# First mixer: matrix powers on a dense form that ScalarE spreads, and scan and output projections in one block by channel halves

## The chip, the cores and the metric

The kernel runs on one core of a Trainium2 chip. The metric is the device time of one execution in microseconds. The program runs two transformer-like blocks over 256 tokens of width 2048; the change touches only the first mixer (S5), which fills the first tenth of the span.

## What is computed

The first mixer, cut to what matters (64 groups of 16 channels, 64 complex states for each group, 256 tokens):

```python
u, z = split(x @ w_in)                      # 2048 -> 2 x 1024
abar = exp(lam * dt)                        # complex, per group and state
bbar = (abar - 1) / lam * b                 # complex 64 x 16 per group
h[t] = abar * h[t-1] + bbar @ u[t]
y = real(c @ h) + d_skip * u
g = gelu(y)
y = g * sigmoid(g @ w_glu + b_glu)
return (y * silu(z)) @ w_out                # then x = layer_norm(alpha * x + ...)
```

## The kernel before

Every projection streams its weights from memory as *pieces* of 128x1024 f32 (512 KB), four to a *tile*. SyncE's queue (SP) loads a piece into one of 3 raw buffers (`stream`, L215) as soon as the difference of the piece three before it is made. ScalarE (ACT) casts it to the rounded half (`high`, L231), VectorE (DVE) forms the bf16 remainder (`low`, L237), and TensorE (PE) does three products for each (L264; L896 for the gate and output projections). 6 slots hold prepared pieces. All engines run their own instruction lists in program order; semaphores are the only tie between them, so the order of the work is the order in which it is written.

`s5_mixer_states` is one block. While PE multiplies the 8 tiles (32 pieces) of the input projection, DVE writes, between its `low` calls, the parameters, the matrices B, AB (`turn_by`, L735 to L740, six operations on 128x1024 each), and a table of cosines and sines that doubles in six steps (L793 to L798). B, A²B and A³B go through `b2`, one after the other: PE turns each (`turn(l)`, L595, 16 transposes into banks 4 to 7), ACT copies it out (`turned_out`, L547), and only then may DVE write the next power into `b2`. The four products of C with powers of A (`turn_conjugate`, L745 to L750) come after the last one. These matrices are block diagonal: a group has 16 channels and the layout gives each state tile 32 columns, so half of the 1024 columns of each part are zeros on either half of the partitions; they are multiplied all the same.

PE then makes `sums(0)` (L605), `kernels` (L619, needs three C powers), after ACT's eight copies of the result (L573, `m_copied`) `sums(1)`, and for each channel half h `direct(h)` (L628) and two `outputs(h, sp)` (L643). DVE runs four scan `unit(h, sp)` (L833 to L849) and two `skip(h)` (L856). A unit other than the first waits for `sums(1)` before it writes its states, since these lie where `sums` reads. The GELU (L580) of a half follows its outputs.

`s5_output` is a second block, behind a barrier of all engines: ACT rounds all of `gel` (L917), DVE forms its remainder (L942), PE does 2 tiles (8 pieces) of the gate projection, ACT the sigmoids (L928), DVE multiplies (L950), ACT rounds (L934), DVE takes the remainder (L952), and PE does 4 tiles (16 pieces) of the output projection. `x_rows` (2 MB, L904) is the first DMA of this block; the first 3 pieces of the gate projection have been loaded since the input projection's end. Layer norm follows in its own block.

Of the kernel before, what the change touches and what calls it, by code (L numbers as in the profile page):

```python
# [20 lines left out]
F32 = mybir.dt.float32  # L21
# [443 lines left out]
S5_GEL, S5_H0, S5_SMALL = 13312, 37888, 38912  # L465


def s5_mixer_states(k):
# [17 lines left out]
    tmp = k.at(S5_TMP, 1024)  # L486
    small = k.at(S5_SMALL, 64)
    k.s5 = dict(small=small)
# [3 lines left out]
    dt_ready, angle, trig, negated = (k.sem(n) for n in "dt_ready angle_ready trig_ready c_negated".split())  # L492
# [16 lines left out]
    with nc.Block() as block:  # L509
        @block.sync  # L510
        def _(sp):
            for n in range(PIECES):
                sp.dma_start(x_raw[:, n * 1024:(n + 1) * 1024],
                             ins["x_t"][:, n * 1024:(n + 1) * 1024]).then_inc(x_in[n], 16)
                if n < RAW:
                    sp.dma_start(k.raw(n), ins["weights"][n]).then_inc(k.landed[n], 16)
                    k.issued += 1
            k.stream(sp, AT_GLU)

        @block.scalar  # L520
        def _(act):
# [16 lines left out]
            for n in range(1, PIECES):  # L538
                high(act, n)
                k.high(act, n)  # L540
            act.wait_ge(bc_in, 64)
            nc.scalar.mul(ct[0][:, 1024:], ct[0][:, 1024:], -1.0).then_inc(negated, 1)
# [6 lines left out]
            for t in range(N_A_IN):  # L549
# [9 lines left out]
                nc.scalar.copy(dst, src).then_inc(k.bank_free, 1)  # L559
                if t == 4:  # L560
                    turned_out(0)
                if t == 6:
                    turned_out(1)
            turned_out(2)
            turned_out(3)
            act.wait_ge(m_sum, 1)
            for h in range(2):
                act.wait_ge(m_clear, h + 1)
                for s in range(4):
# [3 lines left out]
                    nc.scalar.copy(dst, src).then_inc(m_copied, 1)  # L573
            for h in range(2):
# [6 lines left out]
            act.wait_ge(gelu_done, 4)  # L581

        @block.tensor
        def _(pe):
            def turn(l):
# [3 lines left out]
                pe.wait_ge(powers, l + 1)  # L589
# [21 lines left out]
            def kernels():  # L611
                pe.wait_ge(c_powers, STEP - 1)
# [19 lines left out]
            def outputs(h, sp):  # L632
                u = 2 * h + sp
                pe.wait_ge(h_ready, u + 1)
                pe.wait_ge(c_powers, STEP)
# [12 lines left out]
                mm.then_inc(y_sum, 1)  # L648

# [15 lines left out]
            for h in range(2):  # L665
                pe.wait_ge(s_read, h + 1)
                direct(h)
                for sp in range(2):
                    outputs(h, sp)


        @block.vector
        def _(dve):
# [54 lines left out]
            r3 = lambda a: a.rearrange("p (i c) -> p i c", c=32)  # L728
            spread = lambda name: q[name].unsqueeze(2).to_broadcast([P, 32, 32])
            t3 = r3(tmp)  # L730

            def turn_by(out, src, re, im, signal=None):

                (o_r, o_i), (s_r, s_i) = ((r3(a[:, 0:1024]), r3(a[:, 1024:])) for a in (out, src))
                v(tt(o_r, s_r, spread(re), ALU.mult))  # L735
                v(tt(t3, s_i, spread(im), ALU.mult))
                v(tt(o_r, o_r, t3, ALU.subtract))
                v(tt(o_i, s_i, spread(re), ALU.mult))
                v(tt(t3, s_r, spread(im), ALU.mult))
                v(tt(o_i, o_i, t3, ALU.add), signal)  # L740

            def turn_conjugate(out, src, re, im):

                (o_r, o_n), (s_r, s_n) = ((r3(a[:, 0:1024]), r3(a[:, 1024:])) for a in (out, src))
                v(tt(o_r, s_r, spread(re), ALU.mult))  # L745
                v(tt(t3, s_n, spread(im), ALU.mult))
                v(tt(o_r, o_r, t3, ALU.add))
                v(tt(o_n, s_n, spread(re), ALU.mult))
                v(tt(t3, s_r, spread(im), ALU.mult))
                v(tt(o_n, o_n, t3, ALU.subtract), c_powers)  # L750

            dve.wait_ge(bc_in, 64)
            turn_by(bb, b2, "cr", "ci", powers)
# [24 lines left out]
            turn_by(b2, bb, "ar", "ai", powers)  # L778
            low(2)
# [8 lines left out]
            for n in range(6):  # L788
                m = 1 << n
                cc, ss = (q[x].unsqueeze(2).to_broadcast([P, 32, m]) for x in now)  # L790
                t = tmp[:, 0:32 * m].rearrange("p (i t) -> p i t", t=m)
# [7 lines left out]
                low(2 if n >= 3 else 1)  # L799
# [4 lines left out]
            dve.wait_ge(turned, 8)  # L804
            turn_by(b2, bb, "ar2", "ai2", powers)
            low(PIECES * N_A_IN)
            dve.wait_ge(negated, 1)
            v(nc.vector.tensor_copy(flat(q["wc"]), order(q["m4"])))
            dve.wait_ge(turned, 12)
            turn_by(b2, bb, "ar3", "ai3", powers)  # L810

            for d in range(1, STEP + 1):
                n = "" if d == 1 else str(d)
                turn_conjugate(ct[d], ct[0], "ar" + n, "ai" + n)
# [43 lines left out]

            unit(0, 0)
            skip(0)  # L860
            unit(0, 1)
            skip(1)
            unit(1, 0)
            unit(1, 1)


def s5_output(k):

    nc, ps = k.nc, k.ps
    gel, uz, small = k.at(S5_GEL, 2048), k.at(S5_UZ, 4096), k.s5["small"]  # L870
    z = uz[:, 2048:]
    sig, yy, sz = k.at(25600, 2048), k.at(27648, 2048), k.at(29696, 2048)
    gel_parts, yy_parts = k.split_x(35904, 0, 2048), k.split_x(36928, 2048, 2048)
    x, dst = k.at(8192, 4096), k.at(12288, 4096)
    xs, z_done, g_high, g_low, y_done, y_high, y_low, one = (k.sem(n) for n in (
        "x_rows z_silu g_high g_low y_gated y_high y_low glu_piece").split())

    def pieces(pe, first, n, parts, glu):

        for t in range(first, first + n):  # L880
            pe.wait_ge(k.bank_free, t + 1)
            for part in range(PIECES):
                piece = PIECES * t + part
                pe.wait_ge(k.low_done, piece + 1)
                for i, kk, sub in itertools.product(range(3), range(ECH // PIECES), range(4 if glu else 2)):
                    c = part * (ECH // PIECES) + kk
                    if glu:
# [1976 lines left out]
```

## Time and profile before

| | us |
|---|---|
| median of 3 runs | 3306.09 |
| lowest and highest | 3303.09, 3306.78 |
| the profiled execution | 3305.53 |
| its span in the trace | 3303.7 |
| PE, DVE, ACT busy over the span | 93%, 66%, 44% |

The profile's page gives the whole span; the mixer is seen in the windows by stage and in the timelines of the engines. Stages by the trace: input projection to 128 us, matrices and kernels to 172, scan and outputs to 232, gate projection to 272, output projection to 318.

### The profile page before, as it was taken

How to read it: one execution, taken by the hardware profiler on the slowest of the kernel's cores; microseconds unless marked ns; L12 is line 12 of the kernel's file. 1: busy time of each engine (PE TensorE's matmuls, PEld its weight loads, DVE VectorE, ACT ScalarE, POOL GpSimd, SP SyncE). 2: the span in 40 equal slices, each digit the busy share in tenths (PEclk: the TensorE clock that was granted, in tenths of full speed). 3: DMA queues.
4: the chain of work that ended last, by engine and by line, in shares of the span. 5: the costliest groups of instructions: out<-in, count | busy, mean ns of one | idle time of the engine just before them, and what ended most of it. 6: DMA issues, size and time to landing. Idle time of an engine off the chain costs nothing. (4 is left out here: it accounts for less than half of the span.)

```text
span 3303.7 us, 60290 instructions
## 1 busy us (share of the span) xinstructions
PE 3067.2 (93%) x23855; PEld 2517.0 (76%) x23922; DVE 2181.8 (66%) x3042; ACT 1466.8 (44%) x1933; POOL 29.8 (1%) x32
## 2 busy tenths in 40 slices
PE   7677899999988789999979989999999999999997
PEld 6674799988977678999869878777777777777654
DVE  8765544555555685575549999777777777777654
ACT  4223434565652443363434468444444444444443
POOL 0000000000000020000000000000000000000000
PEclk9878899999999899999989999999999999999999
DMA  5214556544435333353545532655566555655554
GB/s 200 77 52 153 199 160 185 166 135 141 139 120 169 128 122 97 116 170 111 178 154 175 175 128 93 215 193 192 186 200 192 191 191 193 198 191 192 191 195 149
DMA packets 143960, 529.90 MB, mean 160 GB/s; under 512 B 16992, under 2 KB 17760, under 8 KB 142048
## 3 DMA queue, kind: packets, MB, share of 16 engines
q1 hardware_dynamic: 140400, 510.33, 47.8%
q10 hardware_dynamic: 3312, 15.92, 1.3%
q8 instruction: 198, 3.24, 0.4%
q14 instruction: 50, 0.41, 0.0%
HBM read 521.99 MB, written 4.19 MB: 159 GB/s over the span
## 5 line engine op out<-in xcount | busy, mean ns | idle before, releaser
L237 DVE TENSOR_TENSOR mem<-mem,rounded 128x1024 bf16<-128x1024 f32 x952 | 1154.2, 1226 | 756.6 <-ACT rounded L231 748.6
L231 ACT CAST rounded<-mem 128x1024 fp32r<-128x1024 f32 x952 | 992.5, 1047 | 1395.4 <-PE ps L264 333.8
L264 PE MATMUL ps<-rounded 128*128 128x256 f32 x3328 | 474.1, 292 | 48.5 <-DVE mem L237 41.7
L264 PEld LDWEIGHTS ps<-rounded 128*128 128x128 f32 x3328 | 422.2, 193 | 53.7 <-issue 22.1
L264 PE MATMUL ps<-rounded,mem 128*128 128x256 bf16 x3328 | 445.5, 280 | 0.0
L264 PE MATMUL ps<-mem,rounded 128*128 128x256 bf16 x3328 | 431.7, 277 | 13.8 <-DVE mem L237 13.8
L264 PEld LDWEIGHTS ps<-mem,rounded 128*128 128x128 bf16 x3328 | 320.7, 99 | 62.8 <-DVE mem L237 8.7
L264 PEld LDWEIGHTS ps<-rounded,mem 128*128 128x128 bf16 x3328 | 316.4, 98 | 62.0 <-issue 1.4
L2444 PE MATMUL ps<-rounded 128*128 128x512 f32 x1024 | 335.3, 441 | 2.1 <-DVE mem L2718 2.1
L2708 DVE TENSOR_TENSOR mem<-mem,ps 128x512 f32<-128x512 f32 x392 | 268.4, 685 | 69.2 <-PE ps L2444 62.5
L2444 PE MATMUL ps<-mem,rounded 128*128 128x512 bf16 x969 | 294.6, 381 | 3.7
L2375 PE MATMUL ps<-rounded 128*128 128x256 f32 x2048 | 288.8, 289 | 8.9 <-ACT mem L2545 3.8
L2375 PE MATMUL ps<-rounded,mem 128*128 128x256 bf16 x2048 | 276.8, 276 | 0.0
L2375 PEld LDWEIGHTS ps<-rounded 128*128 128x128 f32 x2048 | 259.9, 190 | 18.3 <-issue 6.4
L2444 PE MATMUL ps<-rounded,mem 128*128 128x512 bf16 x1016 | 271.2, 387 | 0.5
L2375 PE MATMUL ps<-mem,rounded 128*128 128x256 bf16 x2048 | 247.5, 273 | 1.6 <-DVE mem L237 1.6
L2444 PEld LDWEIGHTS ps<-rounded 128*128 128x128 f32 x1024 | 189.7, 189 | 57.2 <-DVE mem L2718 2.5
L2375 PEld LDWEIGHTS ps<-mem,rounded 128*128 128x128 bf16 x2048 | 199.8, 98 | 27.9 <-DVE mem L237 2.7
L2375 PEld LDWEIGHTS ps<-rounded,mem 128*128 128x128 bf16 x2048 | 187.0, 96 | 36.4
L2444 PEld LDWEIGHTS ps<-rounded,mem 128*128 128x128 bf16 x1024 | 98.8, 97 | 126.5
L2444 PEld LDWEIGHTS ps<-mem,rounded 128*128 128x128 bf16 x1024 | 78.8, 97 | 137.1 <-issue 70.8
L337 PE MATMUL ps<-mem 128*128 128x128 f32 x96 | 18.6, 384 | 72.0 <-DVE mem L422 50.2
(409 smaller groups left out, 2436.8 us busy)
## 6 DMA issues: line engine op xcount, KB each, us to landing
mem<-experts SPq DMA_DIRECT2D x512, 512.0 KB, 3.6
mem<-weights SPq DMA_DIRECT2D x440, 512.0 KB, 3.6
mem<-x_t SPq DMA_DIRECT2D x4, 512.0 KB, 10.1
mem<-x_rows SPq DMA_DIRECT2D x1, 2048.0 KB, 7.5
mem<-ln_g ACTq DMA_DIRECT2D x2, 1024.0 KB, 5.1
mem<-ln_b ACTq DMA_DIRECT2D x2, 1024.0 KB, 7.4
mem<-cmp_w_k ACTq DMA_DIRECT2D x4, 512.0 KB, 5.5
mem<-cmp_w_v ACTq DMA_DIRECT2D x4, 512.0 KB, 4.9
```

What stands on the lines that cost most here:

```text
L231: self.nc.scalar.copy(self.parts(c % SLOTS)[0], self.raw(c % RAW)).then_inc(self.high_done, 1)
L237: self.nc.vector.tensor_tensor(wl, self.raw(c % RAW), wh.bitcast(F32), ALU.subtract).then_inc(self.low_done, 1)
L264: mm = self.nc.tensor.matmul(self.ps[:, bank, half * 256:half * 256 + 256], a, b, start=(part == 0 and n == 0), stop=(part == PIECES - 1 a ...
L337: mm = nc.tensor.transpose(ps[:, b, c * T + tt * P:c * T + tt * P + P], src[:, tt * D + kc * P:tt * D + kc * P + P], self.ident)
L2375: mm = nc.tensor.matmul(ps[:, bank, half * T:half * T + T], a, b, start=(part == 0 and n == 0), stop=(part == PIECES - 1 and n == len(KIND ...
L2444: mm = nc.tensor.matmul(ps[:, bank, :], a, b, start=(j <= WITH_UP and half == 0 and i == 2 * tt), stop=((j < WITH_UP or j == PAIRS - 1) an ...
L2708: nc.vector.tensor_tensor(y[:, a:a + BANK], y[:, a:a + BANK], ps[:, bank, :], ALU.add).then_inc(y_free, 1)
```

## The change

Both functions become one, `s5_mixer`, with one block.

1. **Dense powers.** ACT packs B once and C once into 128x512 a part (`make_dense`, 4 copies of 64x512 each). `turn_by(n)` works on that form, six operations on 128x512, for all eight products: n = 0 and 1 are B and AB, 2 to 5 the four C powers, 6 and 7 A²B and A³B. ACT spreads a result to its place in the wide form (`expand(n)`, 4 copies of 64x512). Two buffers `dense` alternate; from n = 3 on `turn_by(n)` waits until spread n - 2 is done. GpSimd (POOL) clears the five targets that no DMA has filled, once, at the start.
2. **Placement.** The C powers are made inside the table's loop, each followed by two `low` calls, with one instead of one or two before it; spreads stand on ACT behind the drains of tiles 2 to 6.
3. **Waits.** PE's `turn`, `kernels` and `outputs` wait for spreads (`expanded`) instead of DVE's results.
4. **One block by halves.** GELU, rounding, remainder, gate and remainder of the gated product are done for half the channels at a time; a piece of the gate or output projection waits only for the half that it reads. Preparation of the first pieces moves between the units and GELUs. `x_rows` and all pieces behind the first three are issued after the last unit (`h_ready` 4).

```diff
+            def expand(n):
+                act.wait_ge(dense_ready, n + 1)
+                if n == 0:
+                    act.wait_ge(cleared, 5)
+                for l, at_ in ((2, 6), (3, 7)):
+                    if n == at_:
+                        act.wait_ge(turned, 4 * l)
+                for part in range(2):
+                    for f in range(2):
+                        last = nc.scalar.copy(own(SPREADS[n], part, f), dense_of((dense[n % 2], b_dense)[n == 0], part, f))
+                last.then_inc(expanded, 1)
...
+                if t == 1:
+                    make_dense(c_dense, ct[0], c_in_dense)
+                if t == 2:
+                    expand(0)
+                if t == 3:
+                    expand(1)
                 if t == 4:
                     turned_out(0)
+                    expand(2)
+                if t == 5:
+                    expand(3)
                 if t == 6:
                     turned_out(1)
+                    expand(4)
+                    expand(5)
+                    expand(6)
             turned_out(2)
+            expand(7)
             turned_out(3)
...
+            more(3)
+            act.wait_ge(s_sum, 2)
+            nc.scalar.activation(sz, z, ACT.Silu).then_inc(z_done, 1)
             for h in range(2):
                 act.wait_ge(y_sum, 2 * h + 2)
...
+                act.wait_ge(gelu_done, 2 * h + 2)
+                nc.scalar.copy(half(gel_parts[0], h), half(gel, h)).then_inc(g_high, 1)
+                if h == 0:
+                    more(3)
...
-                pe.wait_ge(powers, l + 1)
+                pe.wait_ge(expanded, (1, 2, 7, 8)[l])
...
-                pe.wait_ge(c_powers, STEP - 1)
+                pe.wait_ge(expanded, 5)
...
+                        pe.wait_ge(k.low_done, piece + 1)
+                        pe.wait_ge(low, 1 + part // 2)
...
+        @block.gpsimd
+        def _(pool):
+            for a in (bb, ct[1], ct[2], ct[3], ct[4]):
+                nc.gpsimd.memset(a, 0.0).then_inc(cleared, 1)
...
+            def turn_by(n, src, re, im, conjugate=False):
+                out = (dense[n % 2], b_dense)[n == 0]
+                if n > 2:
+                    dve.wait_ge(expanded, n - 1)
...
-                low(2 if n >= 3 else 1)
+                low(1)
+                if n >= 2:
+                    c_power(n - 1)
+                    low(2)
...
+            for h in range(2):
+                dve.wait_ge(g_high, h + 1)
+                tt(half(gel_parts[1], h), half(gel, h), half(gel_parts[0], h).bitcast(F32), ALU.subtract).then_inc(g_low, 1)
+                more(3 if h == 0 else 2)
...
+            sp.wait_ge(h_ready, 4)
+            sp.dma_start(rows, ins["x_rows"]).then_inc(xs, 16)
+            k.stream(sp, AT_KV)
```

ACT's list at the end of the input projection, before the change (L559 drains a tile, L547 is `turned_out`):

```order
58 L559 COPY mem<-ps 128x512 [waits multiplied]
59 L547 COPY mem<-ps 128x512 [waits b_turned] x4
60 L559 COPY mem<-ps 128x512 [waits multiplied]
61 L547 COPY mem<-ps 128x512 [waits b_turned] x8
62 L573 COPY mem<-ps 32x16x32 [waits s5_kernels_clear,s5_kernels_sum]
```

and after it (L604 drains, L592 is `turned_out`, L582 spreads):

```order
69 L604 COPY mem<-ps 128x512 [waits multiplied]
70 L592 COPY mem<-ps 128x512 [waits b_turned] x4
71 L582 COPY mem<-mem 64x32x16 [waits dense_ready]
72 L582 COPY mem<-mem 64x32x16 x3
73 L582 COPY mem<-mem 64x32x16 [waits dense_ready]
74 L582 COPY mem<-mem 64x32x16 x3
75 L582 COPY mem<-mem 64x32x16 [waits b_turned,dense_ready]
76 L582 COPY mem<-mem 64x32x16 x3
77 L604 COPY mem<-ps 128x512 [waits multiplied]
78 L592 COPY mem<-ps 128x512 [waits b_turned] x4
79 L582 COPY mem<-mem 64x32x16 [waits b_turned,dense_ready]
```

Three spreads now stand between the drain of tile 6 and that of tile 7, and a fourth between the copies of the third and the fourth turned matrix.

DVE's list behind the last `low` of the input projection, before (one operation stands for its group of six; four groups L745 to L750 follow one another):

```order
161 L237 TENSOR_TENSOR mem<-mem,rounded 128x1024 [waits high_done] x4
162 L808 COPY mem<-mem 128x32 [waits c_negated]
163 L735 TENSOR_TENSOR mem<-mem 128x1024 [waits b_turned,vector_step]
...
169 L745 TENSOR_TENSOR mem<-mem 128x1024 [waits b_powers]
...
192 L750 TENSOR_TENSOR mem<-mem 128x1024 [waits vector_step]
193 L817 COPY mem<-mem 128x2048 [waits b_turned,c_powers]
```

and after:

```order
182 L237 TENSOR_TENSOR mem<-mem,rounded 128x1024 [waits high_done] x3
183 L856 TENSOR_TENSOR mem<-mem 128x512 [waits expanded]
...
189 L926 COPY mem<-mem 128x32 [waits dense_ready]
190 L856 TENSOR_TENSOR mem<-mem 128x512 [waits expanded,vector_step]
...
196 L931 COPY mem<-mem 128x2048 [waits b_turned,expanded,dense_ready]
```

Thirty operations on 128x1024 behind the last `low` have become twelve on 128x512.

ACT's list around the two GELUs after the change (L649 rounds a half of `gel`, L231 casts pieces):

```order
92 L647 ACTIVATE mem<-ps 128x2x4x64 [waits s5_y_sum]
93 L647 ACTIVATE mem<-ps 128x2x4x64
94 L649 CAST rounded<-mem 128x1024 [waits s5_gelu]
95 L231 CAST rounded<-mem 128x1024 [waits multiplied,piece_landed_2]
96 L231 CAST rounded<-mem 128x1024 [waits multiplied,piece_landed_0]
97 L231 CAST rounded<-mem 128x1024 [waits multiplied,piece_landed_1]
98 L647 ACTIVATE mem<-ps 128x2x4x64 [waits s5_y_sum]
```

The second GELU stands behind the casts of three pieces whose DMAs are issued behind `x_rows`.

## Rows read from the trace of the kernel before

**Rows 1.** Windows by stage: length, busy time of each engine (instructions), clock, DMA.
```profile
0.00:128.00 128.00, 102.73 (x816) 90.28 (x816) 97.34 (x171) 50.74 (x62) 0.20 (x4) 0.95 0.52 179
128.00:172.00 44.00, 17.39 (x401) 16.35 (x400) 41.84 (x35) 5.46 (x10) 0.00 (x0) 0.71 0.00 1
172.00:232.00 60.00, 55.57 (x928) 55.05 (x928) 43.08 (x52) 7.49 (x10) 0.00 (x0) 0.70 0.01 2
```
**Rows 2.** Timeline of PE, 126 to 240 us: start, length, instruction, idle before.
```profile
126.14 1.91 PE L595 MATMUL ps<-mem 128*128 128x128 f32 x16
135.74 3.68 PE L595 MATMUL ps<-mem 128*128 128x128 f32 x16 [7.68 <-DVE mem L740]
140.09 7.37 PE L605 MATMUL ps<-mem 32*128 32x64 f32 x256 [0.67 <-ACT mem L547]
158.50 6.29 PE L619 MATMUL ps<-mem 128*32 128x128 f32 x128 [11.04 <-DVE mem L750]
174.62 13.93 PE L605 MATMUL ps<-mem 32*128 32x64 f32 x256 [9.82 <-ACT mem L573]
188.48 17.33 PE L628 MATMUL ps<-mem 128*128 128x64 f32 x80
205.74 8.29 PE L643 MATMUL ps<-mem 128*32 128x64 f32 x256
...
223.03 7.15 PE L643 MATMUL ps<-mem 128*32 128x64 f32 x256
```
**Rows 3.** Timeline of DVE: power, table step, last C power, units.
```profile
29.11 1.22 DVE L735 TENSOR_TENSOR mem<-mem 128x1024 f32<-128x1024 f32 x1
...
77.00 0.69 DVE L793 TENSOR_TENSOR mem<-mem 128x512 f32<-128x512 f32 x1
...
164.68 1.23 DVE L750 TENSOR_TENSOR mem<-mem 128x1024 f32<-128x1024 f32 x1
...
171.67 1.16 DVE L833 TENSOR_TENSOR mem<-ps,mem 128x1024 f32<-128x1024 f32 x1
...
183.75 1.22 DVE L833 TENSOR_TENSOR mem<-ps,mem 128x1024 f32<-128x1024 f32 x1
...
216.34 0.68 DVE L849 TENSOR_TENSOR mem<-mem 128x504 f32<-128x504 f32 x1
```
**Rows 4.** Timeline of ACT: drains, copies of turned matrices and of kernels.
```profile
54.28 0.58 ACT L559 COPY mem<-ps 128x512 f32<-128x512 f32 x1
...
119.13 0.58 ACT L559 COPY mem<-ps 128x512 f32<-128x512 f32 x1
119.61 2.05 ACT L547 COPY mem<-ps 128x512 f32<-128x512 f32 x4
...
169.70 4.78 ACT L573 COPY mem<-ps 32x512 f32<-32x512 f32 x8 [29.66 <-DVE mem L819]
```
**Rows 5.** Timelines, gate and output projections: first and last groups.
```profile
238.28 2.05 PE L896 MATMUL ps<-rounded 128*128 128x256 f32 x8 [8.09 <-DVE mem L237]
...
242.87 1.19 PE L896 MATMUL ps<-rounded 128*128 128x256 f32 x8
...
261.30 1.03 PE L896 MATMUL ps<-mem,rounded 128*128 128x256 bf16 x8
271.58 2.08 PE L896 MATMUL ps<-rounded 128*128 128x512 f32 x4 [9.25 <-DVE mem L952]
...
316.40 1.07 PE L896 MATMUL ps<-rounded,mem 128*128 128x512 bf16 x4
```
**Rows 6.** The page, DMA issues: count, KB each, us from issue to landing.
```profile
mem<-weights SPq DMA_DIRECT2D x440, 512.0 KB, 3.6
...
mem<-x_rows SPq DMA_DIRECT2D x1, 2048.0 KB, 7.5
```
**Rows 7.** Timeline of POOL, the shortest and the longest operation there.
```profile
1143.02 0.61 POOL L1911 TENSOR_TENSOR mem<-mem 128x255 f32<-128x255 f32 x1
...
1174.45 2.54 POOL L1911 TENSOR_TENSOR mem<-mem 128x255 f32<-128x255 f32 x1
```

More of the change, by code:

```diff
@@ L573, in _, with more @@
                     nc.scalar.copy(dst, src).then_inc(m_copied, 1)
+            ahead = iter(range(G0, G0 + N_GA))
+            def more(n):
+                for _, c in zip(range(n), ahead):
+                    k.high(act, c)
+            more(3)
+            act.wait_ge(s_sum, 2)
+            nc.scalar.activation(sz, z, ACT.Silu).then_inc(z_done, 1)
             for h in range(2):
@@ L580, in _ @@
                     nc.scalar.activation(dst, src, ACT.Gelu_apprx_tanh).then_inc(gelu_done, 1)
-            act.wait_ge(gelu_done, 4)
+                act.wait_ge(gelu_done, 2 * h + 2)
+                nc.scalar.copy(half(gel_parts[0], h), half(gel, h)).then_inc(g_high, 1)
+                if h == 0:
+                    more(3)
+            for n in range(N_GLU):
+                more(4 if n == 0 else 2)
+                t = AT_GLU + n
+                act.wait_ge(k.multiplied, PIECES * (t + 1))
+                for sub in range(4):
+                    j = 4 * n + sub
+                    last = nc.scalar.activation(sig[:, j * T:(j + 1) * T],
+                                                ps[:, t % BANKS + 3 * (sub // 2), (sub % 2) * T:(sub % 2) * T + T],
+                                               ACT.Sigmoid, bias=small[:, 8 + j:9 + j])
+                    last.then_inc(k.bank_free if sub == 3 else sig_done, 1)
+                act.wait_ge(y_done, n + 1)
+                nc.scalar.copy(half(yy_parts[0], n), half(yy, n)).then_inc(y_high, 1)
+            more(N_GA)
         @block.tensor
@@ L777, in _ @@
             low(2)
-            turn_by(b2, bb, "ar", "ai", powers)
-            low(2)
+            turn_by(1, b_dense, "ar", "ai")
+            low(3)
             order = lambda a: a.rearrange("p (h j s) -> p h s j", h=2, s=4)
@@ L857, in skip, with more @@
                                                      op0=ALU.mult, op1=ALU.add), m_ready if j % 4 == 3 else None)
+            ahead = iter(range(G0, G0 + N_GA))
+            def more(n):
+                for _, c in zip(range(n), ahead):
+                    k.low(dve, c)
             unit(0, 0)
@@ L1409, in first_block @@
 def first_block(k):
-    s5_mixer_states(k)
-    s5_output(k)
+    s5_mixer(k)
     h = k.at(12288, 4096)
```

201 lines of the change are left out of this document (85 added, 116 removed).

## The prediction

> **What bounds the kernel now.** I read the windows by stage first [rows 1]. In the input projection (to 128 us) PE is busy 102.7 of 128 us at a clock of 0.95, and DVE 97.3. From 128 to 172 us PE works 17.4 of 44 us while DVE works 41.8: this stage is DVE's. From 172 to 232 PE works 55.6 of 60 us, at a mean clock of 0.70. The timelines of PE name the holes and who ends them [rows 2]: 7.7 us on the last B power, 11.0 us on the third C power, 9.8 us on the copies of the kernels, and behind the scans 8.1 us on the first pieces of the gate projection and 9.3 us on the remainder of the gated product [rows 5]. The 9.8 us is DVE's too: the copies sat 29.7 us waiting for a memset [rows 4] that stands behind the last C power, which ends at 165.9 us [rows 3].
>
> **1. The powers, up to the end of the input projection.** A power is six operations of 1.22 us, 1.26 us from start to start, so 7.6 us; on 128x512 one takes 0.69 us in the same 32x16 shape with a broadcast operand [rows 3], with the same gap 0.73, so 4.4 us. Ahead of the last `low` DVE had three powers, 22.7 us, and gets six, 26.2 us: +3.5 us of DVE work. Against it stand blocks of 4.4 instead of 7.6 us, which drain PE's prepared pieces less. The two exceptions are the table's last step, now with only one `low` before the next power, and the spreads on ACT. A spread is four copies; the nearest row is four copies of 128x512 in 2.05 us [rows 4]. They lie in ACT's idle time (50.7 busy of 128 us, [rows 1]). I take the last product of the projection at 126.1 us as before, with -4 to +5 us as bounds: minus 4 where the shorter blocks pay, plus 5 for the added DVE work and one more restart at the low clock. POOL's five memsets lie ahead of the first spread and cost nothing here.
>
> **2. From there to `sums(1)`.** New waits come: PE's third turn waits for spread 6. ACT drained tile 6 at 119.1 us and copied four banks in 2.05 us to 121.7 [rows 4]. Spreads 4 and 5 follow to 123.7 and 125.8. DVE's A²B waits for spread 4, its buffer, and takes 4.4: 128.1. Spread 6 ends at 130.2, so the third turn starts there and not at 126.1. PE has idled 4 us; after 7.7 us of idling the same 16 transposes took 3.68 instead of 1.91 us [rows 2], and I take 3.7: 133.9. The last bank is copied at 134.5, spread 7 ends at 136.6, the fourth turn takes 3.7 to 140.3, its last copy 0.7: `sums(0)` starts at 141.1, against 140.1. Up to here the change has lost 1.0 us.
>
> Now the gain. `sums(0)` takes 7.4 us as in its row, to 148.5. The C powers are long spread, so `kernels` follows with no wait. It took 6.29 us after an idle stretch; `sums` shows what the clock makes, 7.37 or 13.93 us [rows 2]. In that ratio full speed is 3.3 us; I take 3.6, with 6.3 as the other end: 152.1. DVE has only a copy and three memsets between its last power (132.5) and the units, so the memsets are done by 146. The eight copies take 4.8 us [rows 4]: `sums(1)` starts at 157.0 instead of 174.6. **Gain 17.6 us.**
>
> **3. `sums(1)` to the last outputs.** Before, this chain is PE's alone: one operation behind the other from 174.62 to 223.03 + 7.15 = 230.2 us, while DVE's last unit ended at 217.0 [rows 2, 3]. PE's idle time ahead of it shrinks from 9.8 to 4.9 us. I take the same durations, which gives 157.0 + 55.6 = 212.6. DVE must not be later: a unit and a skip take 183.75 - 171.67 = 12.1 us [rows 3]. The first unit starts at 148.5; the second, from 160.6, must wait for the end of `sums(1)` at 170.9 before it writes, and ends at 172.6; its skip, three new `low` calls (3.5 us) and two units of 10.5 us end at 198.7. PE wants the last one at about 209. Covered by 10 us.
>
> **4. The hole before the gate projection.** PE goes on at 212.6 with pieces 32 and 33, whose remainders are ready, for 5.5 us, to 218.1. The second half's GELU (2.1), rounding (1.0) and remainder (1.2) end at 217.0. This needs ACT free at 212.6. It stands in three casts whose pieces are issued behind `x_rows` at 198.7. `x_rows` took 7.5 us for 2 MB and a piece lands 3.6 us after its issue [rows 6]. The four transfers are 3.5 MB; in proportion 13.1 us, at best 7.5 + 3 x 1.2 = 11.1. I take 12 and a cast of 1.0: ACT is free at 211.7, by a margin of 0.9 us. So the hole of 8.1 us goes, and with it the restart: the projection took 238.28 to 262.3, 24.0 us [rows 5], of which its last seven pieces took 242.87 to 262.3, 2.78 us each. Eight at that rate take 22.0 with the tail counted once, so the low clock at its start cost 2.0. **Gain 8.1 + 2.0 = 10.1 us**; the gate ends at 234.6.
>
> **5. The hole before the output projection.** The first half's gated product is made while PE does the second gate tile. The second half needs, from 234.6, four sigmoids (1.6), product (1.2), rounding (1.0) and remainder (1.2), 5.2 us with the signals; PE has pieces 40 and 41 to do, 5.4 us. The cover is whole by 0.2 us, and a miss costs what it misses. The output projection took 271.58 to 317.47, 45.9 us, for 16 pieces [rows 5]; at the same price of a restart, 2.0, it takes 43.9 without. **Gain 9.3 + 2.0 = 11.3 us.** It ends at 278.5. Layer norm and all behind it are unchanged and shift as they are. The barrier between the two old blocks was part of the 8.1 us.
>
> Sum: 17.6 + 10.1 + 11.3 = 39.0 us from the profiled execution's 3305.5 (0.6 below the median of the runs): **3266.5 us.**
>
> **The rivals.** *A, the sum as above*, 0.52, within 3262 to 3270.
>
> *B, the clock returns during `sums(1)`.* In the trace PE ran `sums(1)` and `direct(0)` for 31 us without a pause at half speed (13.93 against 7.37, 17.3 us), and sped up in the outputs [rows 2]. If the shorter idle stretch leaves the clock up, PE waits for DVE instead: the units end at 197.4, the outputs at 201.0. But the second GELU still waits for the three pieces, to 210.4; its remainder is there at 214.8, PE has idled 8 us and restarts low, and the end is 277.2: 3265.2. The 11 us that PE gains there are worth 1.3. Chance 0.12. The Trainium skill (TensorE: Matmul & The Clock Gate, Part 1: The HAM clock gate) says that sustained matmul activity releases the low clock soon after its start; the rows of `sums(1)` and `direct(0)` speak against it. By that rule the time would be this rival's.
>
> *C, the clock is low in `sums(0)`.* The third and fourth turns now stand apart, each after a pause, where one pair stood before. If the clock has not risen by 141 us, `sums(0)` takes 13.9 and `kernels` 5.3: +8.2 us on everything behind, 3275. Chance 0.14.
>
> *D, the fetch behind `x_rows` is late.* If the four transfers take 16 us, ACT is free at 215.7, PE stops for 2.5 us and may restart low: 3270 to 3272. Chance 0.08.
>
> *E, the input projection gets longer*, by the 3.5 us of DVE work and spreads that hold back casts, plus a low restart: 3271 to 3274. Chance 0.09.
>
> *F, slower: POOL's memsets.* Spread 0 waits for all five and stands on ACT at 54.8 us [rows 4]; behind it are the casts of tile 4 and so the whole projection. Five clears of 2048 columns have no row. From operations on 255 columns in 0.61 to 2.54 us [rows 7], eight times as wide: 24 to 102 us together. Up to 54 us they are free; beyond, each us delays all. At 93 us, 18.6 us each, the gain is gone; at 102 us the result is 3314. Those rows have two operands to read and a memset has none, so I stay near the short end. Chance 0.03. The Trainium skill (SBUF — State Buffer, Who interferes with whom) says that a DVE operation with two inputs contends with GpSimd operations that read, and not with ones that only write; no run shown here has both, and by it the clears disturb nobody.
>
> The last 0.02 is for a spread that costs far more than its row.
>
> **How the numbers follow.** A and B are the two likeliest and lie together. C, D and E reach to 3275. Bounds: 4 us off the projection below, 5 above. The range 3257 to 3277 leaves out F and the sums of two mishaps, some 2 in 10. About 0.2% is what a measurement of this kernel can tell from no change, 7 us: even C is 31 us below the old time. Faster 0.95, within 0.2% 0.02, slower 0.03.
>
> **What the new profile would show.** PE's first `sums` near 141 us and `kernels` right behind it; the second near 157, at half the clock; no gap over 1 us between the last outputs and the last product of the output projection, at about 278.5. A gap in the third and fourth gate pieces means B or D; `sums(0)` of 14 us means C; POOL busy beyond 54 us means F. I am wrong in kind if DVE's `low` calls wait for ACT's spreads in the projection, for which the last product there would lie beyond 131 us.

## The result, and the profile after

The changed kernel takes 3271.95 us (median of 4 runs, 3266.00 to 3273.36) against 3306.44 us before (4 runs, 3303.09 to 3309.07): a ratio of 0.9896, 95% interval 0.9884 to 0.9908. It is faster by 34.5 us where 39.0 were forecast; the forecast time was 3266.5, its range 3257 to 3277. The profiled execution took 3271.05 us, its span is 3269.3.

The timeline of PE after the input projection, columns as in [rows 2]:

```profile
132.52 3.61 PE L678 MATMUL ps<-mem 128*128 128x128 f32 x16 [6.34 <-ACT mem L582]
139.33 3.62 PE L678 MATMUL ps<-mem 128*128 128x128 f32 x16 [3.20 <-ACT mem L582]
143.63 11.65 PE L688 MATMUL ps<-mem 32*128 32x64 f32 x256 [0.68 <-ACT mem L592]
155.21 5.99 PE L702 MATMUL ps<-mem 128*32 128x128 f32 x128
166.20 13.93 PE L688 MATMUL ps<-mem 32*128 32x64 f32 x256 [4.99 <-ACT mem L631]
180.06 17.33 PE L711 MATMUL ps<-mem 128*128 128x64 f32 x80
...
215.12 7.15 PE L726 MATMUL ps<-mem 128*32 128x64 f32 x256
222.20 1.21 PE L753 MATMUL ps<-rounded 128*128 128x256 f32 x8
...
244.20 1.17 PE L753 MATMUL ps<-rounded 128*128 128x512 f32 x4
```

Where PE stood 7.7 us ahead of the fourth turn and 11.0 ahead of `kernels` [rows 2], it now stands 6.3 and 3.2 ahead of the third and fourth turn and not at all ahead of `kernels`; the 9.8 us ahead of `sums(1)` are 5.0; those of 8.1 and 9.3 us ahead of the two projections [rows 5] are gone. But `sums(0)` takes 11.65 us where it took 7.37. The windows of that stretch say why (from:to, length, busy time of PE, PEld, DVE, ACT, POOL, granted clock of PE, DMA):

```profile
144.00:146.00 2.00, 2.00 (x80) 2.00 (x80) 1.41 (x3) 0.00 (x0) 0.00 (x0) 1.00 0.04 8
146.00:148.00 2.00, 2.00 (x49) 2.00 (x48) 1.62 (x2) 0.00 (x0) 0.00 (x0) 0.55 0.00 0
148.00:160.00 12.00, 12.00 (x234) 11.70 (x233) 5.43 (x6) 0.00 (x0) 0.00 (x0) 0.51 0.01 3
160.00:164.00 4.00, 1.21 (x44) 0.94 (x34) 3.90 (x4) 2.64 (x5) 0.00 (x0) 0.91 0.00 0
164.00:200.00 36.00, 33.80 (x388) 33.60 (x390) 30.83 (x40) 9.39 (x10) 0.00 (x0) 0.50 0.01 1
...
202.00:222.00 20.00, 20.00 (x488) 19.84 (x485) 10.18 (x11) 6.23 (x6) 0.00 (x0) 1.00 0.52 192
```

The clock (0.5 is 1.2 GHz, 1.0 is 2.4) fell at 146 us, in the middle of `sums(0)`, while PE was fully busy. It stayed at half through `sums(1)` and `direct(0)`, 36 us with PE busy for 33.8 of them, and was full again at 202.

ScalarE's timeline shows the price of a spread (four copies of 64x512, L582), what stands ahead of the spreads, and how the second GELU stands behind the three late casts:

```profile
119.72 1.05 ACT L231 CAST rounded<-mem 128x1024 fp32r<-128x1024 f32 x1 [5.63 <-DMA mem<-weights]
120.67 0.58 ACT L604 COPY mem<-ps 128x512 f32<-128x512 f32 x1
121.15 2.05 ACT L592 COPY mem<-ps 128x512 f32<-128x512 f32 x4
123.06 5.04 ACT L582 COPY mem<-mem 64x512 f32<-64x512 f32 x8
129.97 2.50 ACT L582 COPY mem<-mem 64x512 f32<-64x512 f32 x4 [1.86 <-DVE mem L861]
...
220.10 1.05 ACT L231 CAST rounded<-mem 128x1024 fp32r<-128x1024 f32 x1 [0.18 <-DMA mem<-weights]
222.32 2.02 ACT L647 ACTIVATE mem<-ps 128x512 f32<-128x512 f32 x2 [1.17 <-PE ps L726]
```

Tile 6 is drained at 120.67 us, behind the cast of a piece whose load ended late; before the change it was drained at 119.13 [rows 4].

Last, POOL's five clears, against which [rows 7] had to serve as a bound:

```profile
0.74 8.77 POOL L787 MEMSET mem<- 128x2048 f32 x5 [0.29 <-POOLq L2904]
```

| PE, us | before | forecast | after |
|---|---|---|---|
| input projection ends | 126.1 | 126.1 | 126.1 |
| third turn starts | 126.1 | 130.2 | 132.5 |
| `sums(0)` starts, length | 140.1, 7.4 | 141.1, 7.4 | 143.6, 11.65 |
| `kernels`, length | 6.3 | 3.6 | 6.0 |
| `sums(1)` starts | 174.6 | 157.0 | 166.2 |
| last outputs end | 230.2 | 212.6 | 222.3 |
| gate projection ends | 262.3 | 234.6 | 244.2 |
| output projection ends | 317.5 | 278.5 | 288.0 |

### The profile page after: what moved, and what is told of

The parts are those of the page before. It is cut to its first block and busy times, and to the rows that moved or that the text cites. A ratio compares the mean times of both kernels' runs of the same rounds, so it can differ in the third digit from the quotient of the medians.

```text
span 3269.3 us, 60355 instructions
## 1 busy us (share of the span) xinstructions
PE 3063.5 (94%) x23855; PEld 2516.6 (77%) x23922; DVE 2158.3 (66%) x3046; ACT 1490.4 (46%) x1975; POOL 38.6 (1%) x37
## 3 DMA queue, kind: packets, MB, share of 16 engines
q8 instruction: 198, 3.24, 0.4%
## 5 line engine op out<-in xcount | busy, mean ns | idle before, releaser
L231 ACT CAST rounded<-mem 128x1024 fp32r<-128x1024 f32 x952 | 991.8, 1047 | 1376.5 <-PE ps L264 335.3
L264 PEld LDWEIGHTS ps<-mem,rounded 128*128 128x128 bf16 x3328 | 318.6, 99 | 66.0 <-DVE mem L237 17.5
L337 PE MATMUL ps<-mem 128*128 128x128 f32 x96 | 17.0, 358 | 70.0 <-DVE mem L422 48.6
```

The lines of the kernel that those rows point to most:

```text
L231: self.nc.scalar.copy(self.parts(c % SLOTS)[0], self.raw(c % RAW)).then_inc(self.high_done, 1)
L264: mm = self.nc.tensor.matmul(self.ps[:, bank, half * 256:half * 256 + 256], a, b, start=(part == 0 and n == 0), stop=(part == PIECES - 1 a ...
L337: mm = nc.tensor.transpose(ps[:, b, c * T + tt * P:c * T + tt * P + P], src[:, tt * D + kc * P:tt * D + kc * P + P], self.ident)
```

## The experiments

**One part alone.** `powers_only` keeps the old order of blocks and takes the new powers; `halves_only` the reverse.

```diff
 powers_only: s5_mixer with the dense powers, spreads and clears; then, in a block of its own as before,
+    s5_output(k)
 halves_only: one block by halves, powers on 128x1024 by VectorE alone
-            make_dense(dense[1], b2, b_in_dense)
...
-            r3 = lambda a: a.rearrange("p (i c) -> p i c", c=16)
+            r3 = lambda a: a.rearrange("p (i c) -> p i c", c=32)
```

> Powers in the dense form, with spreads, as in the changed kernel; the output stage is the old one, a block of its own behind a barrier. Theory (the two parts add): PE's timeline up to the last outputs is that of the changed kernel (first sums near 143.6 us and 11 to 12 us long, last outputs ending near 222.3), then the two old holes of 8.1 and 9.3 us and the two restarts at the low clock, 21.4 us together: 21.4 us above the changed kernel's 3272.0, 3293.4. Rival 1: the 4.9 us by which the changed kernel's profiled execution is ahead of what its mixer saves belong to run-to-run differences; then this one gains only the 7.9 us of the earlier last outputs on 3306.4: 3298.5. Rival 2: the spreads and added waits bring nothing without the halves: 3306.

> The old wide powers on VectorE, with no spreads and no memsets on GpSimd; scan and output stage in one block by halves, as in the changed kernel. Theory (fetch coupling): last outputs end near 230.2 us; VectorE's last unit ends at 217.0 plus 3.5 for three new differences, 220.5, x_rows is issued there, its three followers have landed and been cast 13.2 us later at 233.7, so the second GELU starts 3.5 us after its sums are ready and the third gate piece waits 2.4 us: 21.4 less 2.4 gained, 3287.4. Rival: the fetch does not matter, 21.4 gained, 3285.0, with no gap in the gate projection. Rival 2: the halves were worth less and the rest came from the powers: above 3292.

Powers alone: 3297.62 us (8 runs, 3289.39 to 3300.98), ratio 0.9970 (0.9958 to 0.9982). Halves alone: 3282.89 us (4 runs, 3280.62 to 3283.51), ratio 0.9931 (0.9914 to 0.9947). The two ratios multiply to 0.9901, and both parts together have 0.9896: within the intervals the parts add. The powers alone came out 4.2 us above their theory (3293.4) and near their first rival; the halves alone 2.1 below the rival that the fetch does not matter (3285.0), and their gate projection runs without a gap. Timeline of PE with the powers alone:

```profile
144.22 13.93 PE L659 MATMUL ps<-mem 32*128 32x64 f32 x256 [0.67 <-ACT mem L588]
158.08 5.40 PE L673 MATMUL ps<-mem 128*32 128x128 f32 x128
168.44 13.93 PE L659 MATMUL ps<-mem 32*128 32x64 f32 x256 [4.97 <-ACT mem L627]
...
232.30 2.04 PE L978 MATMUL ps<-rounded 128*128 128x256 f32 x8 [8.09 <-DVE mem L237]
```

Here `sums(0)` ran wholly at half clock, the powers gained 6.2 us instead of 17.6, and the old hole of 8.09 us stands as it was. The eight runs lie in two groups, three at 3289.4 to 3291.2 and five at 3295.6 to 3301.0; the mean clock was 0.962 to 0.964 in the first three and 0.960 in the four longest. That is the size of what the clock does to `sums(0)` and `kernels`, up to 8.2 us by the prediction's rows, but only one of the eight has rows, so this reading is argued, not shown. The halves alone went from last outputs at 232.2 to a gate's end at 254.1: the time from the last outputs to the layer norm's transposes (L337, which start at 339.25 us before the change) was 109.1 us before, 87.8 with the halves alone and 87.2 in the changed kernel. The prediction's steps 4 and 5 said 21.4 less; it is 21.3 and 21.9.

**Keeping the clock up.** Transposes of the identity into a free bank, in PE's pauses: 76 ahead of `sums(0)`, or 40 ahead of `sums(1)`.

```diff
 fill_sums0
+            filler(50)
             turn(2)
+            filler(26)
             turn(3)
 fill_sums1
             pe.wait_ge(k.bank_free, AT_A_IN + N_A_IN + BANKS)
+            filler(40)
             pe.wait_ge(m_copied, 8)
             sums(1)
```

> The changed kernel with 76 needless 128x128 transposes of the identity into a free bank, 50 ahead of the third turn and 26 ahead of the fourth, so that PE doesn't pause there (the result is unaffected). Theory 1 (the pauses before it made the clock fall in the first sums): the turns take 1.9 us each, sums(0) starts near 140.3 us and takes 7.4, kernels 3.6, sums(1) starts near 156.2: 10 us gained, 3262. Theory 2 (the products of sums, 32 rows deep, do not hold the clock, whatever ran before): sums(0) starts near 140.3 but its second part is again at half the clock, 9 to 12 us in all, kernels 6: 2 to 5 us gained, 3267 to 3270.

> The changed kernel with 40 needless 128x128 transposes between kernels and sums(1), where PE pauses 5.0 us. Theory 1 (the pause brings the clock down): sums(1) takes 7.4 us and direct(0) 9.1 instead of 13.9 and 17.3, the last outputs then wait for VectorE's units, and the second GELU for its three casts: last outputs 10 us earlier, but a hole in the gate projection; end 1 to 5 us earlier. Theory 2 (sums doesn't hold the clock): sums(1) starts at full speed and loses it on the way, 9 to 12 us, direct(0) at half speed, 17.3: last outputs 2 to 5 us earlier.

Ahead of `sums(0)`: 3287.32 us (2 runs), 15 slower than the changed kernel. Ahead of `sums(1)`: 3271.29 (2 runs), no difference. Both times mislead. Windows of the first, then PE's timeline of the second:

```profile
126.00:140.00 14.00, 12.48 (x112) 11.92 (x110) 8.44 (x13) 11.11 (x20) 0.00 (x0) 1.00 0.01 1
140.00:142.00 2.00, 1.17 (x38) 1.02 (x39) 1.31 (x2) 0.93 (x2) 0.00 (x0) 1.00 0.00 0
...
144.00:154.00 10.00, 10.00 (x192) 9.85 (x192) 3.04 (x3) 0.00 (x0) 0.00 (x0) 0.50 0.01 2
```

```profile
143.79 7.37 PE L688 MATMUL ps<-mem 32*128 32x64 f32 x256 [0.68 <-ACT mem L592]
...
159.76 7.37 PE L688 MATMUL ps<-mem 32*128 32x64 f32 x256 [0.38 <-ACT mem L631]
167.06 9.14 PE L711 MATMUL ps<-mem 128*128 128x64 f32 x80
...
217.98 2.05 PE L753 MATMUL ps<-rounded 128*128 128x256 f32 x8 [6.76 <-DVE mem L994]
```

In the first the clock was full from 126 to 142 us and still fell early in `sums(0)` (11.66 us), as its theory 2 had it. But that theory's reason, that the products of `sums` do not hold the clock, falls with the second kernel, where `sums(0)` and `sums(1)` both ran in 7.37 us. There all is at full clock from 144 to 200, `direct(0)` took 9.14 us, and the outputs ended 16.8 us earlier, at 205.5. Not all of that is the fillers' work: `sums(1)` began 6.4 us earlier than in the changed kernel, because `sums(0)` and `kernels` ahead of the fillers, whose code is the same in both, ran at full clock in this execution. Some 10 us are left for the fillers. Then the gate projection stopped for 6.8 us on the second half's remainder, whose GELU stands behind the late casts; the layer norm's transposes came 8.3 us earlier (301.1), and 1.4 earlier in the first kernel. Up to here neither kernel is later than the changed one, but the first lost 16 us and the second 8 somewhere behind 310 us.

**Where the fillers' time went.** Both lost most of it (15.0 and 6.3 us) between the pauses of PE at 2001.5 and 3077.3 us (in the changed kernel's time), in the expert stage, where the same code runs. The timeline of PE in that stage, of `fill_sums0`:

```profile
2289.92 1.22 PE L2427 MATMUL ps<-rounded 128*128 128x256 f32 x8 [1.03 <-issue]
2293.19 0.86 PE L2427 MATMUL ps<-rounded,mem 128*128 128x256 bf16 x6 [1.81 <-issue]
```

"issue" is a wait for nothing that the profile shows; such waits come back once per expert, every 133 us. The next two kernels add 40 or 128 small transposes (32x32) in the middle of the input projection:

```diff
             turn(0)
+            pad(40)    # or pad(128)
```

> The changed kernel with 40 small transposes (32x32, into a PSUM bank that nothing uses then) on TensorE behind the turning of B, in the middle of the input projection, where TensorE waits for VectorE anyway. What is computed stays the same. It asks why the kernels with fillers lost time in the expert stage, 1500 us behind the fillers: between the pauses at 2001.5 and 3077.3 the changed kernel takes 1075.8 us, the one with 40 fillers ahead of the second sums 1082.1, the one with 76 fillers 1090.8, and there TensorE stands still for 1 to 2 us, with no releaser, once per expert. Theory P: what counts is where TensorE's later instructions lie in its stream; 40 more matmuls (80 instructions) shift them as before, so the stretch takes 1080 to 1084 us and shows such pauses, and the whole 3275 to 3279 us. Theory Q: the fillers' place and kind made it (they ran beside the first mixer's end, and changed when later transfers start): here the stretch takes 1075 to 1077 us and the whole 3269 to 3273.

> The same with 128 small transposes in place of 40, at the same place: 256 more instructions in TensorE's stream. One expert's work is 1152 matmuls, 2304 instructions or 9 times 256, and the pauses came back at one place of each expert; if the stream is loaded in blocks of 256 instructions, a shift by 256 puts every later instruction where it was. Theory P (place in the stream, in blocks of 256): the stretch in the expert stage takes 1075 to 1077 us again and has no such pauses, the whole 3269 to 3273 us. If more instructions cost more of themselves, the stretch takes over 1090 and the whole over 3285. Theory Q: 1075 to 1077 too, so this run tells P from 'more is worse', and the run with 40 tells P from Q. The 128 transposes take 3.5 to 7 us of TensorE beside pauses of 28.9 us in all: nothing of it should reach the projection's end at 126.1.

They took 3271.25 us (3267.17 and 3275.33) and 3268.39 (3264.35 and 3272.44). The two runs of each lie 8 us apart, too far to tell one theory from the other. The stretch in the trace, from one execution of each kernel, tells more:

| instructions added on PE | stretch in the expert stage, us |
|---|---|
| none (before, changed, five others here) | 1075.8 to 1077.9 |
| 80 (`fill_sums1`, `pad40`) | 1082.1, 1079.9 |
| 152 (`fill_sums0`) | 1090.8 |
| 256 (`pad128` and three below) | 1076.6 to 1077.7 |

`pad40` has the waits again, `pad128` none of 0.9 us or more:

```profile
2554.23 1.21 PE L2425 MATMUL ps<-rounded 128*128 128x256 f32 x8 [1.22 <-issue]
```

So with 80 or 152 more instructions ahead of it the unchanged stage took 2 to 15 us more, and with 256 more it did not: what counts is the place of PE's later instructions in its stream, not how many were added. Of these rows `pad40` is weak, since it lies 2.0 us above the unshifted kernels, one execution of it has a trace, and `powers_only` and `rows_twice`, which add nothing, have such waits too, of up to 1.0 us. A second sign of the place is a pause in the last outputs, shown below with `rows_twice`. That it is the loading of instructions in blocks fits, but is not shown. The page has a queue for it (`q8 instruction`, 198 packets, 3.24 MB), with 199 packets in all four kernels with 256 more but 200 in `fill_sums0`; no row ties a packet to a wait, and the block could as well be a divisor of 256. With 256 in all (`fill_pad`: 40 ahead of `sums(1)`, `pad(88)` in the projection):

> The changed kernel (powers in its own order) with the 40 transposes ahead of the second sums and 88 small ones behind the turning of B, 256 instructions in all. It separates the two things that the run with 40 alone mixed: its output projection ended 8.2 us earlier, its expert stage took 6 us more. Theory: granted clock 1.00 from 144 to 200, gate projection done at 236, expert stretch 1076 to 1078 us, and the whole 3262 to 3266 us, 6 to 10 us under the changed kernel. Rival: the gain of the clock is given back elsewhere whatever the place in the stream, and the whole stays within 3 us of 3271.

3267.05 us (4 runs, 3263.08 to 3268.16), ratio 0.9882 (0.9865 to 0.9898), 4.9 less than the changed kernel and between its theory and its rival; the runs of the two kernels overlap. `sums(0)` was at half clock this time (13.93 us), `sums(1)` at full (7.37). The outputs ended at 209.5, 12.8 us earlier, the gate projection at 242.4, only 1.8 earlier. This is rival B's price: PE's gain is held by the three pieces behind `x_rows`.

**The load of `x_rows`.**

```diff
+            for o in (S5_TMP, S5_B2):
+                sp.dma_start(k.at(o, 2048), ins["x_rows"][:, 0:2048]).then_inc(xs, 16)
             sp.dma_start(rows, ins["x_rows"]).then_inc(xs, 16)
```

> The changed kernel with two more loads of 1 MB (halves of x_rows, into buffers that are free by then and that nothing reads) ahead of the load of x_rows; VectorE waits for all three where it waited for x_rows. It asks whether the load of x_rows, which stands ahead of the gate projection's weight pieces 35 to 37 in the queue, is really hidden, and by how little. In the changed kernel those pieces are cast at 217.6 to 221.1, the second GELU, queued behind them on ScalarE, ends its wait with 1.2 us to spare, and the gate projection runs without a gap. Two more MB at the rate of x_rows itself (2 MB in 7.4 us) put the pieces about 7 us later. Theory: the second GELU and the low part of its halves follow, the gate projection stops for 5 to 6 us between its second and third pieces and starts again at the lower clock, and the whole takes 5 to 8 us more than the changed kernel: 3277 to 3280 us. Rival: the pieces have slack that the profile doesn't show, and the whole stays within 2 us of 3272.

3275.53 us (4 runs, 3275.30 to 3278.38), 3.6 more: between both. ScalarE cast the first of the three pieces 5.4 us later:

```profile
222.97 1.04 ACT L231 CAST rounded<-mem 128x1024 fp32r<-128x1024 f32 x1 [13.56 <-DMA mem<-weights]
```

But the gate projection did not stop for it, since PE came late too, by a pause in the last outputs, while 4 MB were being fetched:

```profile
224.50 0.82 PE L728 MATMUL ps<-mem 128*32 128x64 f32 x17 [2.55 <-issue]
```

Three more kernels have this pause, and its place tells of PE's stream. It stands 17 matmuls before the end of the outputs in `rows_twice` (2.55 us) and `halves_only` (1.61), 93 before it in `fill_sums0` (1.21), which has 76 more ahead, and 57 before it in `pad40` (0.21), which has 40 more ahead: at one place by count, wherever that falls in the code. Why it is longest beside the larger fetch was not tested.

In `rows_twice` it made the outputs end 3.0 us later and the gate projection, restarted at the low clock, take 1.3 us more. So the margin of 1.2 us was neither used up nor proved; the extra traffic cost what it did in another way.

**An order without the pauses.** The table above shows 17.5 us between the projection and `sums(0)`, all of them two spreads, two turns and their copies. `early` brings A²B and A³B forward: nothing is computed anew. The edit, condensed and without VectorE's part:

```diff
-    SPREADS = (bb, b2, ct[1], ct[2], ct[3], ct[4], b2, b2)
+    SPREADS = (bb, b2, b2, ct[1], b2, ct[2], ct[3], ct[4])
 ScalarE, behind the drain of tile 4, 5, 6
+                if t == 4: turned_out(0); turned_out(1); expand(2)
+                if t == 5: expand(3); turned_out(2); expand(4)
+                if t == 6: turned_out(3); expand(5); expand(6)
 TensorE
+            for l in range(1, STEP):
+                k.multiply(pe, AT_A_IN + 3 + l, 1, xT, "channel")
+                turn(l)
+            k.multiply(pe, AT_A_IN + 7, 1, xT, "channel")
```

> The changed kernel with the powers in another order: A2B right behind AB, then AC, A3B, A2C, A3C, A4C; ScalarE spreads A2B and A3B during tiles 4 and 5 and copies out every turned power as it comes; TensorE turns one power behind each of tiles 4, 5 and 6, in place of the last two behind the projection. The same numbers are computed. Theory: the 17.5 us from the projection's end at 126.1 to the first sums at 143.6 were the wait for two spreads (6.3 and 3.2), two turns at the lower clock (3.6 each) and their copies (0.7), all of which now lie inside the projection, whose last wait for VectorE is at 114.97. Projection's end 126 to 129 (two turns of 1.9 us are now inside it), first sums at 127 to 130, that is 14 to 16.5 us earlier; VectorE's first unit starts when the sums are done, at 135 to 141 in place of 155.3, and since what follows is the chain sums, kernels, sums, outputs, the last outputs end 14 to 19 us earlier (203 to 208) and the whole takes 3253 to 3259 us. Rival: the casts and low parts of the weights, which the spreads now delay on ScalarE, hold the projection back: its end moves to 132 or later, the whole to 3262 or more. Rival 2: the projection is followed by the sums without a pause and the clock behaves otherwise: full through sums and kernels, 6.6 us less than that, or half from the start, 2.3 us more.

3248.34 us (4 runs, 3246.86 to 3249.26), ratio 0.9821 (0.9804 to 0.9837), 23.6 less than the changed kernel:

```profile
126.29 7.37 PE L688 MATMUL ps<-mem 32*128 32x64 f32 x256
133.59 3.77 PE L702 MATMUL ps<-mem 128*32 128x128 f32 x128
142.33 13.93 PE L688 MATMUL ps<-mem 32*128 32x64 f32 x256 [4.97 <-ACT mem L631]
```

`sums(0)` now follows the projection without a pause, 17.3 us earlier and at full clock; the outputs end at 198.3, the gate projection at 220.2. It gained more than its theory, because the clock held in `sums(0)` and `kernels`: that is its rival 2, which put 6.6 us on it. Three more kernels add the fillers (40 and 88), a later load of `x_rows`, or both:

```diff
 x_rows behind the gate projection's pieces
-            k.stream(sp, AT_GLU)
+            k.stream(sp, AT_A_OUT)
             sp.wait_ge(h_ready, 4)
             sp.dma_start(rows, ins["x_rows"]).then_inc(xs, 16)
```

> The kernel with the earlier powers, with 40 transposes of 128x128 ahead of the second sums, where TensorE waits 5 us for ScalarE's copies of the kernels (they kept the granted clock at 1.00 all through the sums, the direct part and the outputs in the earlier run with them, where those ended 16.8 us earlier), and 88 small transposes behind the turning of B, so that 256 instructions in all are added to TensorE's stream and the expert stage is left as it was by the theory of blocks of 256. Theory: clock full from the second sums on, last outputs no longer bound by TensorE at half clock but by VectorE's units, end of the gate projection 224 to 228 (235.96 with the 40 alone, less the 10 to 14 us that the units start earlier), expert stretch 1075 to 1077; the whole 3247 to 3254 us. Rivals: the gate projection is held by its weights and VectorE's low parts and ends as in the kernel with earlier powers alone, the whole within 2 us of it; or the clock falls in the first sums and stays low in spite of the fillers: the same, within 2 us.

> The kernel with earlier powers and both kinds of transposes, with one more change: SyncE issues the gate projection's weight pieces 35 to 42 first, as their slots come free, and waits for the scan and loads x_rows behind them. In the two earlier kernels pieces 35 to 37 were cast at 195 us in both, though TensorE had finished the outputs at 198.3 in one and 191.0 in the other: they stood behind the wait for VectorE's last unit (184.8) and the 7.4 us of x_rows, and so the gate projection ended at 220.2 and 221.4. Theory: the pieces' slots are free at 164, they are cast before 175, the gate projection starts at 191 and runs without a gap, 22.0 us, to 213, 8 us earlier; x_rows is issued by about 205 and there long before the output projection's first end at 237; the whole takes 3240 to 3244 us. Rival: the output projection's own pieces (eight of 512 KB, fetched over 38 us) are held by the load of x_rows, which now falls among them, and give 3 to 8 us of it back: 3244 to 3250 us.

> The kernel with earlier powers and the load of x_rows behind the gate projection's pieces, without any transposes added. The transposes alone gave nothing (3249.4 against 3248.3 us), both together 8.5 us (3239.8). Theory: without them TensorE does the second sums and the first direct part at the lower clock and finishes the outputs at 198.3, when pieces 35 to 37 are cast in either order, so the gate projection ends at 220.2 as before and the whole takes 3247 to 3249 us: the two cuts are worth something only together. Rival: the load's place is worth its 8 us by itself, 3240 us, and the transposes do nothing.

| | median (4 runs), us | outputs end | gate projection ends |
|---|---|---|---|
| `early` | 3248.34 | 198.3 | 220.2 |
| `early_fill` | 3249.40 | 191.1 | 221.4 |
| `early_rows` | 3249.09 | 199.8 | 221.7 |
| `early_fill_rows` | 3239.84 (3239.21 to 3240.73) | 191.4 | 213.3 |

Either alone is worth nothing, both together 8.5 us. `early_fill` came out as its rival had it, the other two as their theories did, within 0.2 us of their ranges. With the fillers alone ScalarE's casts of pieces 35 to 37 are late; with both they are there, and the load of `x_rows`, which lands in 9.4 us, is issued 30 us before VectorE first reads it (230.3). First ScalarE of `early_fill`, then ScalarE and SyncE's queue of `early_fill_rows`:

```profile
195.08 1.05 ACT L231 CAST rounded<-mem 128x1024 fp32r<-128x1024 f32 x1 [24.71 <-DMA mem<-weights]
```

```profile
170.58 2.93 ACT L231 CAST rounded<-mem 128x1024 fp32r<-128x1024 f32 x3
...
199.88 0.42 SPq L543 DMA_DIRECT2D mem<-x_rows  x1
```

`early_fill_rows` beats both kernels: ratio 0.9803 (0.9786 to 0.9819) to the one before, 32 us less than the changed one. What binds it now is VectorE's last unit (PE waits 4.8 us for it ahead of the last outputs).

## Why the prediction was right, and where its steps were not

The forecast was 5.4 us too low, and the mechanism was the one that it named: PE's holes in front of the chain and in front of the two projections went. Its largest term was not right, and part of what that term missed came back by a gain that nobody had forecast.

**Step 1** held for the end of the input projection, 126.1 us. Over the first 126 us VectorE was busy for 102.3 us where it had been 97.3, more than the 3.5 us expected. PE was busy for 97.1 instead of 100.7, at a mean clock of 0.97 instead of 0.95, so it ran less of its work at the low clock. That shorter blocks did this fits, but no run separates them. The spreads fit into ScalarE's idle time.

**Step 2** is where the 9.2 us by which `sums(1)` was late come from, in three terms. First, `sums(0)` started 2.5 us late. Of this 1.4 us was there before any spread began, since the drain of tile 6 stood behind a late cast and came at 120.67 us instead of 119.1. Most of the rest is the spreads: each was sized by four copies of 128x512 from PSUM, 2.05 us, and four of 64x512 within SBUF took 2.50. Second, `sums(0)` was taken at 7.4 us and was 11.65 (+4.3). Third, `kernels` was taken at 3.6 and was 5.99 (+2.4, close to the other end, 6.3). Rival C named the last two, with a chance of 0.14 and a price of 8.2 us; they came to 6.7. Its mechanism was that the clock has not risen by 141 us. It had risen (1.00 from 144 to 146) and fell again in a busy stretch, which no rival held. In `powers_only`, whose code up to there is the same, it had not risen. The gain of the step was 8.4 us, not 17.6.

**Step 3** held in all its durations: 166.2 + 56.1 = 222.3, where 55.6 were taken. VectorE was covered: its second unit waited 3.9 us for `sums(1)`, as the step said it would. In `fill_sums1`, where PE was faster, the cover was gone, and PE waited 4.1 us for the last unit, as rival B had it.

**Steps 4 and 5** held. Forecast 21.4 us, measured 21.9 up to the layer norm and 21.3 with the halves alone. The margin of 0.9 us for the second GELU was 1.2. The gate projection took 22.0 us. Rival D did not come about. Where PE was ahead, in `fill_sums1`, `fill_pad` and `early_fill`, the gate projection did stop for the three late casts, for 6.8, 8.5 and 6.2 us: that is rival B's price, with a fetch of about the length forecast.

**Rival F** fell: 8.8 us for five clears, 1.75 each, where the rows allowed 24 to 102.

**The sum** was 9.5 us too low at the end of the output projection, and 4.6 at the end of the span, where 34.4 us were gained of the 39.0 (5.4 against the median, as the forecast started 0.9 us below it). That it came so close is luck in part. The layer norm's transposes came 29.8 us earlier and the end of the span 34.4. From L337's start to the end it takes 2964.5 us before and 2965.3 with the powers alone, but 2958.8 to 2961.8 in the nine kernels with the merged block and no shift of 80 or 152 instructions. That the merged block makes these 3 to 6 us, far behind it, is argued from one execution of each. By the pauses of PE they gather in small steps: counted from L337's start the changed kernel is 1.9 us ahead after 750 us, 3.4 after 1361 and 5.5 after 1629. The cause was not found, and no step of the prediction had them.

## What to carry to other kernels

Ahead of a chain that one engine runs alone, pull every short serial step (a copy, a turn, its drain) under the last work that has slack: here 17 us came from the order of eight products, nothing else. A cut on the engine that waits is worth only as much as the next releaser allows, so test two cuts together before either is dropped: fillers and a later load gave 0 and 0 alone, 8.5 us together. And when a small edit changes the time of a stage it doesn't touch, compare that stage in both traces before the edit is blamed.

## What the runs showed of the hardware

- The same code had three lengths of `sums(0)`. With no difference in PE's code ahead of it, it took 7.37 us in `fill_sums1`, 11.65 in the changed kernel, 11.60 in `rows_twice` and 13.93 in `powers_only`: a profile shows one draw. Of the ten profiled kernels with a pause ahead of it, two ran it in 7.4 us (full clock), four in 11.6 (it fell on the way), four in 13.9 (half). In the four kernels where it follows the projection without a pause it took 7.37 each time.
- With 40 transposes in the pause ahead of `sums(1)` it took 7.37 us in all four kernels that have them, and 13.93 in all ten that don't. A fully busy PE at half clock did not bring the clock back for 34 us (166 to 200). The Trainium skill (TensorE: Matmul & The Clock Gate, Part 1: The HAM clock gate) says that sustained matmul activity releases the low clock soon; by these rows it did not, and what PE did in the pause ahead of the stretch decided.
- Copies of 64x512 within SBUF on ScalarE took 0.62 us each, no less than 128x512 from PSUM (0.58).
- GpSimd cleared 128x2048 f32 in 1.75 us (five in 8.77).
- 80 or 152 instructions added on PE between 64 and 160 us made unchanged code from 2001 us on 2 to 15 us longer, and 256 added instructions did not. A pause in the last outputs stood at one place of PE's stream by count in four kernels, whatever was added ahead.
